# A two-layer decoder trunk: gate matrices from bf16 one-hots, shorter candidate lists, bf16 look-ups and an earlier start of the late tiles

## What is computed

```python
q = (xb @ w_q).reshape(P_BLOCK, P_HEADS, P_QDIM)           # 8 heads of 2 x 128
s1 = einsum('thd,nd->thn', q[..., :128], k1); s2 = ...     # 128 scores for each half
v1, i1 = top_k(s1, 16); v2, i2 = top_k(s2, 16)
cand = v1[..., :, None] + v2[..., None, :]                 # 16 x 16 sums a head
cand_id = i1[..., :, None] * 128 + i2[..., None, :]
top_s, pos = top_k(cand, 16); eid = take_along_axis(cand_id, pos)
gate = softmax(top_s)
act = gelu(einsum('thkd,td->thk', u_tab[eid], xb))
out = einsum('thk,thkd->td', gate * act, v_tab[eid])
```

## Time and profile before

| | us |
|---|---|
| median of 3 runs | 1986.55 |
| lowest and highest | 1984.23, 1987.65 |
| the profiled execution: device time | 1984.32 |
| its span in the profile | 1982.6 |
| TensorE busy in the span | 1937.8 (98%) |
| VectorE, ScalarE, GpSimd busy | 1346.4, 1069.0, 270.8 |
| granted TensorE clock, share of full speed | 0.995 |

### The profile page before, as it was taken

The page is one execution under the profiler, slowest core; times in us unless marked ns, Lnnn a source line. Parts: engine busy times, 40 slices in busy tenths (PEclk is TensorE's granted clock), DMA queues, the critical chain, the costliest instruction groups (busy, mean ns, idle before and its releaser), DMA issues.

```text
span 1982.6 us, 38964 instructions
## 1 busy us (share of the span) xinstructions
PE 1937.8 (98%) x12552; PEld 1768.7 (89%) x12552; DVE 1346.4 (68%) x2319; ACT 1069.0 (54%) x1848; POOL 270.8 (14%) x122
## 2 busy tenths in 40 slices
PE   7989999999999999999999899999999999999998
PEld 6778999999999888888888699999999998888886
DVE  5764859478888666666658659574888876666666
ACT  4534444566666544555455544445666665545554
POOL 0113780200000000000006068420000000000000
PEclk9999999999999999999999999999999999999999
DMA  7744455544444555555544344555444445555554
GB/s 257 240 140 147 150 186 185 180 159 138 138 138 139 191 193 195 192 190 192 195 156 135 127 149 160 180 189 179 141 138 138 138 159 191 193 196 193 191 192 147
DMA packets 92805, 338.80 MB, mean 171 GB/s; under 512 B 10384, under 2 KB 10512, under 8 KB 92240
## 3 DMA queue, kind: packets, MB, share of 16 engines
q1 hardware_dynamic: 90864, 329.49, 50.1%
q0 software_dynamic: 1888, 8.62, 1.3%
HBM read 337.02 MB, written 1.05 MB: 171 GB/s over the span
## 4 chain that ended last, share of the span: by engine, by line
PE 86%; DVE 5%; POOL 4%; issue 3%; ACT 1%; DMA 0%; POOLq 0%; DVEq 0%; ACTq 0%
PE psum L1069 86%; POOL tile_lo L367 4%; DVE tile_lo L695 1%; DVE hn L727 1%; DVE hT_lo L736 0%; DVE zv L788 0%; DVE qe L1005 0%; ACT tile_hi L438 0%; DMA gain_row<-in_gains 0%; DVE zu L797 0%; DVE ke L1006 0%; DVE x L748 0%; DVE zu L762 0%; DVE score_in L1017 0%; DVE yT_lo L803 0%
## 5 line engine op out<-in xcount | busy, mean ns | idle before, releaser
L695 DVE TENSOR_TENSOR tile_lo<-raw,tile_hi 128x1024 fp32r<-128x1024 f32 x548 | 676.2, 1234 | 296.9 <-ACT tile_hi L438 296.4
L438 ACT ACTIVATE tile_hi<-raw 128x1024 fp32r<-128x1024 f32 x624 | 655.9, 1051 | 357.7 <-PE psum L1069 354.7
L1069 PE MATMUL psum<-hT_hi,tile_hi 128*128 128x256 f32 x2368 | 592.6, 289 | 1.2 <-ACT tile_hi L438 1.1
L1069 PE MATMUL psum<-hT_lo,tile_hi 128*128 128x256 f32 x2368 | 577.7, 283 | 2.3 <-DVE hT_lo L736 2.3
L1069 PEld LDWEIGHTS psum<-hT_hi,tile_hi 128*128 128x128 f32 x2368 | 452.0, 192 | 3.4 <-issue 1.4
L1069 PEld LDWEIGHTS psum<-hT_lo,tile_hi 128*128 128x128 f32 x2368 | 451.9, 191 | 3.0 <-DVE hT_lo L736 3.0
L1069 PE MATMUL psum<-hT_hi,tile_lo 128*128 128x256 f32 x2368 | 333.0, 283 | 3.7 <-POOL tile_lo L367 3.7
L1069 PEld LDWEIGHTS psum<-hT_hi,tile_lo 128*128 128x128 f32 x2368 | 305.4, 192 | 4.9 <-POOL tile_lo L367 4.9
L572 ACT ACTIVATE w_hi<-acts 128x256 fp32r (+1 forms) x256 | 106.8, 418 | 341.6 <-PE psum L1069 340.8
L1069 PE MATMUL psum<-tile_hi,w_hi 128*128 128x512 f32 x1024 | 274.0, 389 | 0.0
L1069 PE MATMUL psum<-tile_hi,w_lo 128*128 128x512 f32 x1024 | 274.0, 389 | 0.0
(11 more groups left out here) (178 smaller groups left out, 1353.1 us busy)
## 6 DMA issues: line engine op xcount, KB each, us to landing
raw<-in_u SPq DMA_DIRECT2D x256, 512.0 KB, 3.3
raw<-in_v SPq DMA_DIRECT2D x256, 512.0 KB, 3.2
raw<-in_a_in SPq DMA_DIRECT2D x32, 512.0 KB, 4.4
raw<-in_w_q SPq DMA_DIRECT2D x32, 512.0 KB, 3.2
raw<-in_a_out SPq DMA_DIRECT2D x16, 512.0 KB, 3.3
raw<-in_b_rv SPq DMA_DIRECT2D x16, 512.0 KB, 3.2
raw<-in_b_qk SPq DMA_DIRECT2D x8, 512.0 KB, 3.3
raw<-in_b_out SPq DMA_DIRECT2D x8, 512.0 KB, 3.3
```

The source lines that it names most:

```text
L438: act.activation(tile_hi[slot % SPLIT_SLOTS][:, :], raw[slot][:, :], ACT.Copy).then_inc(hi_ready, 1)
L695: dve.tensor_tensor(tile_lo[s][:, :], raw[slot][:, :], tile_hi[s][:, :].bitcast(F32), ALU.subtract).then_inc(lo_ready, 1)
L1069: return pe.matmul(o, a, b, start=start, stop=stop, skip_group_check=True)
```

## The change

1. **Gate matrices.** VectorE writes both one-hots of a group at once, in bf16 (`hot`, one instruction of 1024 elements). The weight is cut into three bf16 pieces: `w_top` (scaled on ScalarE into `top_hot`) and `w16` (two pieces, `low_hot`, one instruction of 1024 elements on VectorE). TensorE adds three bf16 products for each token, 12 a group, in place of four fp32 ones. Three PSUM banks serve the groups instead of four.
2. **Late tiles.** `EARLY` is 40, so 88 tiles are late; in a turn of eight tiles, tiles 0, 1, 2, 4, 5 and 6 carry a group. `EXP_AT` is 28, `TURN_AT` 32.
3. **Candidates.** The four best rows are joined with all 16 of the other half, the other twelve with the best 4: 64 + 48 = 112 sums a head instead of 256.
4. **Look-ups.** They run in bf16 for both token halves at once (4096 elements), and the sum over ranks is made by halving adds instead of a reduce. No low part stands between them; all stand before VectorE's first low part, and GpSimd makes the low parts up to tile 27 (`POOL_U` = 28).
5. **Scores** are copied two rows at a time, for both halves together.

```diff
-EXP_AT = 48
-TURN_AT = 52
-N_LATE = GROUPS
-EARLY = NK - N_LATE
-POOL_U = 24
+EXP_AT = 28
+TURN_AT = 32
+EARLY = 40
+N_LATE = NK - EARLY
+POOL_U = 28
+LATE_STEP = 8
+GROUP_AT = (0, 1, 2, 4, 5, 6)
+GATE_BANKS = 3
+WIDE, WIDE_ROWS = 4, 4
+NARROW = 4
+CANDS = WIDE_ROWS * TOPK + (TOPK - WIDE_ROWS) * NARROW
...
-                pool.wait_ge(shifted[l], TT)
+                pool.wait_ge(looked[l], 2)
                 pool.memset(acts[:, EARLY:N_EXP, :], 1.0).then_inc(ones_ready[l], 1)
...
-                        eq = did(dve.tensor_tensor(look[:, :, :, :], want, ranks, ALU.is_equal))
-                        lo_at(n)
-                        n += 1
-                        after(eq)
-                        eq = did(dve.tensor_tensor(look[:, :, :, :], look[:, :, :, :], numbers, ALU.mult))
-                        n = two_tiles(n)
-                        after(eq)
-                        eq = did(dve.tensor_reduce(picks[:, h, half, :].rearrange("p (g k) -> p g k", g=P_HEADS),
-                                                   look[:, :, :, :], AX.X, ALU.add))
+                full = [P, TT * P_HEADS, TOPK, TOPK]
+                for half, pos in ((0, pos_a), (1, pos_b)):
...
+                    ranks = rank16[:, :, :].unsqueeze(1).broadcast_to(full)
+                    numbers = topi16[:, :, :, :].rearrange("p h (g s) r -> p (h g) s r", s=2)[:, :, half, :].unsqueeze(3).broadcast_to(full)
+                    after(did(dve.tensor_tensor(look[:, :, :, :], pos[:, :, :].unsqueeze(2).broadcast_to(full), ranks, ALU.is_equal)))
+                    after(did(dve.tensor_tensor(look[:, :, :, :], look[:, :, :, :], numbers, ALU.mult)))
+                    for m in (8, 4, 2):
+                        after(did(dve.tensor_tensor(look[:, :, 0:m, :], look[:, :, 0:m, :], look[:, :, m:2 * m, :], ALU.add)))
+                    ends = look[:, :, 0:2, :].rearrange("p (h g) r k -> p h g r k", h=TT)
+                    dve.tensor_tensor(picks[:, :, half, :].rearrange("p h (g k) -> p h g k", g=P_HEADS),
+                                      ends[:, :, :, 0, :], ends[:, :, :, 1, :], ALU.add).then_inc(looked[l], 1)
+                n = UT[l] + POOL_U
                 while n < UT[l] + 2 + EXP_AT:
                     lo_at(n)
...
+                    s = g % 2
                     for c in range(GROUP):
-                        ins = product(psum[:, 4 + g % 4, c * P:(c + 1) * P], onehot1[:, g % 2, c, :], onehot2[:, g % 2, c, :],
-                                      start=True, stop=True)
+                        o = psum[:, 4 + g % GATE_BANKS, c * P:(c + 1) * P]
+                        product(o, hot[:, s, 0, :, c], top_hot[:, s, c, :], start=True)
+                        product(o, hot[:, s, 0, :, c], low_hot[:, s, 0, :, c])
+                        ins = product(o, hot[:, s, 0, :, c], low_hot[:, s, 1, :, c], stop=True)
                     ins.then_inc(gmat_done[l], 1)
```

More of the change, by code:

```diff
@@ L929, in late_product @@
                     dve.tensor_tensor(place, place, gelu_out[:, c % 2, :], ALU.mult).then_inc(late_gated[l], 1)
                 def late_tile(i, c, first, last):
-                    if not (first and c < 2):
-                        dve.wait_ge(late_gated[l], i * RAW_SLOTS + (c - 1))
-                    gate(i * (RAW_SLOTS * GROUP) + c * GROUP, c, i * RAW_SLOTS + (c + 1))
-                    if not (last and c + 2 >= RAW_SLOTS):
-                        onehot(i * (RAW_SLOTS * GROUP) + (c + 2) * GROUP, c % 2)
@@ L949, in peer @@
-                dve.wait_ge(numbers_ready, 1)
-                for g in range(4):
-                    equal(g * GROUP, g % 2, g - 1 if g >= 2 else None)
-                    if g == 1:
-                        for k in range(first_onehots + 2, EARLY + 1):
-                            lo_at(UT[l] + k)
+                    g = GROUP_AT.index(c) if c in GROUP_AT else None
+                    if last and g is not None and (LATE_STEPS - 1) * STEP_GROUPS + g >= GROUPS:
+                        g = None
@@ new lines, in late_tile @@
+                    more = g is not None and not (last and (LATE_STEPS - 1) * STEP_GROUPS + g + 2 >= GROUPS)
+                    token2 = None if g is None else i * (STEP_GROUPS * GROUP) + (g + 2) * GROUP
+                    if g is not None:
+                        if not (first and c < 2):
+                            dve.wait_ge(late_gated[l], i * LATE_STEP + (c - 1))
+                        gate(i * (STEP_GROUPS * GROUP) + g * GROUP, 4 + g % GATE_BANKS, i * STEP_GROUPS + (g + 1))
+                        if more:
+                            hot_pair(token2, g % 2)
@@ new lines, in late_tile @@
+                    n = UT[l] + 1 + EARLY + c
+                    lo(n % RAW_SLOTS, i * LATE_STEP + (n + 1))
+                    if not (first and c == 0):
+                        gates = i * STEP_GROUPS + sum(at <= c for at in GROUP_AT)
+                        late_product(i, c - 1, min(gates, GROUPS) if last else gates)
+                    if more:
+                        low_pair(token2, g % 2, i * STEP_GROUPS + (g + 3))
+                dve.wait_ge(picksT_ready[l], 3)
+                hot_pair(0, 0)
@@ new lines, in late_tile @@
+                def late_tile(i, c, first, groups):
+                    if c in GROUP_AT and GROUP_AT.index(c) < groups:
+                        gate_matrices(i, GROUP_AT.index(c), first)
+                    t = i * LATE_STEP
+                    pe.wait_ge(gelu_done[l], t + (EARLY + c + 1 - RAW_SLOTS))
+                    stationary_tile(c % 2, t + (UT[l] + EARLY + c + 1), c % RAW_SLOTS, (lo_ready, t + (late + c)))
+                for c in range(LATE_STEP):
+                    late_tile(0, c, True, STEP_GROUPS)
@@ L1246, in value_tile @@
+                with pe.Fori(1, LATE_STEPS - 1) as i:
+                    for c in range(LATE_STEP):
+                        late_tile(i, c, False, STEP_GROUPS)
+                for c in range(LATE_STEP):
+                    late_tile(LATE_STEPS - 1, c, False, GROUPS - (LATE_STEPS - 1) * STEP_GROUPS)
                 def value_tile(slot, ready, rest_ready, k, start, stop, half=None):
```

273 lines of the change are left out of this document (139 added, 134 removed).

## The result

| | before | changed |
|---|---|---|
| median, us | 1985.57 (4 runs) | 2042.84 (4 runs, 2042.49 to 2045.51) |
| span of the profiled execution | 1982.6 | 2040.8 |
| TensorE, VectorE busy | 1937.8, 1346.4 | 1981.3, 1414.2 |
| granted clock | 0.995 | 0.994 |

The changed kernel is slower by 57.3 us, ratio 1.029 (95% interval 1.0273 to 1.0308). 1997 was forecast, with 2032 as the upper end. The spans of the two profiled executions differ by 58.2.

A forecast was written before the change was run, and what follows sets the result against it. The prediction took TensorE's own work as the bound. From 1984.3 us, groups -11.1 and early stage +21.4, late tiles zero, gave 1994.6 for the profiled execution and a median of 1997 us; range 1968 to 2032.

The forecast's parts named there:

- The bound: Whole kernel: TensorE alone, without a gap from 247.19 us to the end in the first peer; second layer the same.
- the two thin places: Late tiles: VectorE waits 0.62 to 0.67 us for TensorE; early stage: GpSimd needs 2.40 of each 2.88 us.
- The groups: Gate matrices on TensorE: twelve bf16 products take 0.80 us a group against 0.887, -11.1 us, bounds -25 and +57.
- rival 2: Groups on TensorE: products at 57.7 ns, 0.69 us a group, 1983 us in all; chance 0.12.
- Rivals 3: Groups on TensorE: weight loads no longer fully covered, 1.0 us a group, 2022 us in all; chance 0.20.
- rival 4: Groups on TensorE: the weight load paces wholly, 0.111 us each, 1.33 a group, 2065 us in all; chance 0.12.
- The late tiles: 88 late tiles: VectorE's and ScalarE's work hidden behind TensorE; zero cost, up to +3 us a layer.
- The early stage: Candidates and look-ups: VectorE takes turns with GpSimd's low parts, look-ups end at 320.2; +10.8 us a layer, +21.4 for two.
- The sign named for them: Early stage: GpSimd's low parts at about 4.6 to 6.8 us in place of 2.40 beside VectorE's look-ups.
- the first rival: Early stage: 16-bit look-ups take no turns with GpSimd, -2.5 us a layer, 1970 us in all; chance 0.14.
- The sum: Whole kernel: 1984.3 - 11.1 + 21.4 = 1994.6 us for the profiled execution, median 2.2 above it, 1997 us.
- The range: Whole kernel: 1968 to 2032 us with 0.8 or a little more inside, the weight load's full pace left out.

The follow-up runs named there:

- run 2: Changed kernel with the moving operand of the two low-piece products taken as 128 elements side by side, for timing only: 1985.4 us.
- run 1: Changed kernel with the weights of all three products of a token taken as 128 elements side by side, for timing only: 2040.9 us.
- Runs 3: Kernel before with parts 3 to 5 of the change alone (POOL_U = 28), its groups and late tiles kept: 2005.6 us, ratio 1.010.
- run 4: Kernel before with parts 3 to 5, GpSimd's low parts only to tile 15, look-ups by token half between VectorE's low parts: 1980.65 us, ratio 0.9971.
- run 6: Changed kernel with low_hot packed for TensorE, VectorE writing it with tokens innermost, 256 bytes apart: 2404.3 us.

## Why the prediction was wrong

**The bound** was right: TensorE alone, in every stretch, and the two thin places were the right ones to look at.

**The groups** failed, and with them the number. The step was the pace of a bf16 product: 0.067 us was taken, for all twelve. Measured are 0.057 for the four with a packed moving operand and 0.120 for the eight with a step of 8 bytes, 1.19 us a group in place of 0.80. The term was -11.1 us and is +38.8. Of the bounds, 0.69 and 1.33, the truth lies between, but for a reason that stands nowhere in the prediction: it asked what the columns, the overhead and the weight load cost and never looked at how the operands lie. No row of before showed it, since its fp32 `onehot2` is packed, as are the operands of the experts; the diff did (`low_hot[:, s, 0, :, c]`, with c the last of the dimensions). Had all been packed, a group would have cost 0.74 (run 2), halfway between rival 2's 0.69 and the forecast's 0.80: the pace within the group is rival 2's, 0.057, not the 67 ns preferred for the company of the expert products, and the edge adds 0.06 that neither had. The Trainium skill ("TensorE: Matmul & The Clock Gate", Back-to-back issue gap) has about 56 ns for the isolated product of 128 columns and about 81 in a sustained stream of load and product. In this stream, twelve at a time between expert products, the packed ones went at 57.

**Rivals 3 and 4**, the weight load as pace, gave 2022 and 2065, and the result lies between them but comes from another cause. A bf16 load takes 0.117 us and not 0.192, is covered even by products 0.057 apart, and its own layout changes next to nothing (run 1).

**The late tiles**: right. VectorE still waits 0.71 to 0.77 us for TensorE, though TensorE's longer group has a part in that; the low pieces take 0.68 us, as long as `hot`, which is 0.59 from the next instruction where 0.6 was reckoned; the 24 more late tiles go at 2.88, and the setting to one takes 18.94 us where 19 was reckoned.

**The early stage**: right, and somewhat too dear: +8.6 and +9.8 us in the two layers against +10.8 (10.7 in the sum). Each duration held (candidates, best 16s, multiply 4.4, adds); the line ran ahead of the forecast by 3 us at the candidates (244.98, not 248) and by 6 at the first look-up (273.31, not 279.4), as the small instructions before the look-ups lost some 8 us to low parts and not 11.1. One of those that waited has a single input, which the reckoning had left out (0.29 of its own). It started just behind a low part; its like, L875, started 0.01 us ahead of that low part and wasn't held (timelines of VectorE and GpSimd):

```profile
267.63 0.29 DVE L875 TENSOR_SCALAR part<-candpos 128x256 uint32<-128x256 uint32 x1
267.64 2.54 POOL L381 TENSOR_TENSOR tile_lo<-raw,tile_hi 128x1024 fp32r<-128x1024 f32 x1 [0.34 <-ACT tile_hi L452]
267.83 2.50 DVE L876 TENSOR_SCALAR part<-candpos 128x256 uint32<-128x256 uint32 x1
```

The look-ups ended at 313.4, not 320.2, and lay beside eleven low parts, not nine. The sign named for them, low parts of 4.6 to 6.8 us, held for few: the four from 273.40 on take 17.05 together, the six from 294.02 on 21.65. Runs 3 and 4 show that it is their place beside GpSimd's low parts that costs, 19 us for the two layers, and 25 against the spread order. That the turns hold for 16-bit operands too, which the first rival doubted, is in the rows: 6.49 for a multiply that took 2 x 2.28 in halves in run 4, 2.52 for an add of 0.43. With the rule of the Trainium skill ("SBUF — State Buffer", Who interferes with whom) on VectorE instructions with two SBUF inputs beside a GpSimd instruction that reads SBUF, these rows agree, as those of before did.

**The sum** had two terms, and the error is the first: 1984.3 + 38.8 + 21.4 would have been 2044.5 for the profiled execution, which took 2042.5.

**The range** reached to 2032 since rival 4 was left outside it. Its bounds had 1.33 us a group, and a cost without any row of its own should have stayed in the range up to that bound.

## What to carry to other kernels

Before a product is priced by its columns, look at the step of its moving operand: here 128 bf16 elements 8 bytes apart cost twice as much as packed ones, 16 bytes apart four times, and 4 bytes apart next to nothing. Choose a layout in which the engine that writes and the one that reads both go along it. Where that can't be had, letting VectorE read across by 8 bytes and write along (1.22 us) was far cheaper here than reading along and writing across by 256 (4.80). Instructions of VectorE with two SBUF inputs are better placed where GpSimd makes no low parts, fp32 and bf16 alike; moved under GpSimd's subtractions, ten of twelve lost about one low part each.

## What was not expected of the hardware

- The moving operand's step: 128 bf16 elements take 0.057, 0.060, 0.120 and 0.228 us at steps of 2, 4, 8 and 16 bytes; weights read at a step of 8 bytes cost next to none (2 us of 2043 at most, one execution).
- VectorE's write with a step of 256 bytes: 4.80 us for 1024 bf16 elements, 1.22 with the output packed and an input at a step of 8 bytes, 0.68 where output and one-hot both lie in runs of four neighbours.
- A single-input instruction of VectorE on uint32 (L876 above) took turns with GpSimd too, 2.50 us for 0.29; in run 4, with GpSimd idle, the same instruction takes 0.29.
- In run 6 TensorE waits for VectorE, and its granted clock falls: 0.940 over the span, and 0.87, a mean of its two levels (1.2 and 2.4 GHz), from 480 to 640 us, where it is busy 112 of 160 us (in the changed kernel 1.00, the upper level, and all of it). VectorE is busy for 158.8 of these 160 us, and its work alone accounts for run 6's loss (429 us reckoned, 419 measured), so nothing there shows a cost of the clock.
